# Attention of a hybrid inference step: nine of ten key tiles turned by DMA, the ninth together with the reciprocals

## The reference

```python
C_HEADS = 8; QK_NOPE = 64; QK_ROPE = 32; V_DIM = 64      # 1024 sample keys + 256 cached keys; 128 prompt keys
s  = einsum('bqhd,bkhd->bhqk', q, k) * ATTN_SCALE
pr = softmax(s, axis=-1)
o  = einsum('bhqk,bkhd->bqhd', pr, v)
...
mixed = concatenate([out_a, out_b, o]); x = x + g1 * (mixed @ w_out)
```

## Time and profile before

| | us |
|---|---|
| time, median of 3 runs | 1522.87 (1521.13 to 1523.97) |
| the profiled execution's own time | 1522.13 |
| its span | 1520.2 |
| TensorE busy | 1480.5 |
| VectorE, ScalarE, GpSimd busy | 605.1, 408.0, 280.3 |

### The profile page before, as it was taken

How to read it: one execution, slowest core, us unless ns; L and a number is a source line. 1 busy time by engine, 2 the same in 40 slices (tenths; PEclk the granted TensorE clock), 3 DMA queues, 4 the chain that set the end, 5 groups by cost and what they waited for, 6 DMA issues and landing times.

```text
span 1520.2 us, 25562 instructions
## 1 busy us (share of the span) xinstructions
PE 1480.5 (97%) x10145; PEld 1180.3 (78%) x10145; DVE 605.1 (40%) x1385; ACT 408.0 (27%) x933; POOL 280.3 (18%) x308
## 2 busy tenths in 40 slices
PE   6999999999999999999999999999999999999997
PEld 3654545666666655444899999999999999999996
DVE  2211446676868673136683222222222222222215
ACT  2400102555646452235321111111111111111114
POOL 0005400463747463110000100100000000000000
PEclk9999999999999999999999999999999999999999
DMA  9971001475747593541587999999889989899885
GB/s 364 353 261 50 32 0 41 82 137 104 142 98 144 130 200 73 194 166 70 191 322 271 323 294 312 315 353 300 291 316 296 362 293 300 313 292 357 291 260 223
DMA packets 313917, 338.79 MB, mean 223 GB/s; under 512 B 209091, under 2 KB 210666, under 8 KB 311678
## 3 DMA queue, kind: packets, MB, share of 16 engines
q1 hardware_dynamic: 308814, 319.58, 66.4%
q0 software_dynamic: 4752, 17.30, 4.4%
q10 hardware_dynamic: 288, 1.05, 0.2%
HBM read 266.18 MB, written 21.64 MB: 189 GB/s over the span
## 4 chain that ended last, share of the span: by engine, by line
PE 88%; DVE 5%; DMA 4%; ACT 2%; issue 1%; POOL 0%; SPq 0%; DVEq 0%; ACTq 0%; POOLq 0%
PE ps L1286 32%; PE ps L1315 16%; PE ps L678 8%; PE ps L1016 7%; PE ps L915 6%; PE ps L969 4%; DMA wreg<-wreg 2%; PE ps L703 2%; PE ps L869 2%; PE ps L693 1%; PE ps L894 1%; PE ps L881 1%; DVE stat L1921 1%; PE ps L710 1%; DMA wreg<-x_rows 1%
## 5 line engine op out<-in xcount | busy, mean ns | idle before, releaser
L1286 PE MATMUL ps<-mreg,wreg 128*128 128x144 f32 x4096 | 506.3, 286 | 0.0
L1286 PEld LDWEIGHTS ps<-mreg,wreg 128*128 128x128 f32 x4096 | 503.4, 190 | 0.7 <-ACT hreg L1625 0.4
L1315 PE MATMUL ps<-mreg,wreg 128*128 128x144 f32 x2048 | 256.4, 286 | 2.1 <-DVE mreg L2365 2.1
L1315 PEld LDWEIGHTS ps<-mreg,wreg 128*128 128x128 f32 x2048 | 253.1, 190 | 2.5 <-DVE mreg L2365 2.3
L2365 DVE TENSOR_TENSOR mreg<-ps,mreg 128x144 f32<-128x144 f32 x128 | 39.4, 307 | 357.6 <-PE ps L1286 346.7
L2530 POOL COPY wreg<-hreg 128x1024 uint16<-128x1024 uint16 x128 | 146.2, 1168 | 156.7 <-ACT hreg L1504 156.1
L915 PE MATMUL ps<-wreg 128*128 128x512 f32 (+2 forms) x400 | 159.0, 520 | 3.8 <-ACT hreg L1504 3.7
L1662 ACT ACTIVATE mreg<-ps 128x144 f32<-128x144 f32 x128 | 37.2, 291 | 426.1 <-PE ps L1286 426.1
L1016 PE MATMUL ps<-wreg,mreg 128*128 128x512 f32 x288 | 130.5, 598 | 0.0
L678 PE MATMUL ps<-hreg,wreg 128*128 128x512 f32 (+1 forms) x400 | 128.9, 480 | 0.0
L2577 POOL DMA_INDIRECT x_rows<-hreg,idx_s x15 | 23.9, 1596 | 533.1 <-DVE hreg L2342 521.6
(11 more groups left out here) (310 smaller groups left out, 1217.7 us busy)
## 6 DMA issues: line engine op xcount, KB each, us to landing
wreg<-in_w_e_dram SPq DMA_DIRECT2D x96, 2048.0 KB, 12.4
wreg<-in_w_ada_dram SPq DMA_DIRECT2D x16, 1024.0 KB, 8.3
wreg<-in_w_ada_dram SPq DMA_DIRECT2D x16, 512.0 KB, 10.9
wreg<-in_w_out_dram SPq DMA_DIRECT2D x8, 512.0 KB, 4.2
wreg<-in_x_sample_dram SPq DMA_DIRECT2D x8, 512.0 KB, 4.6
x_rows<-wreg SPq DMA_DIRECT2D x8, 512.0 KB, 3.5
xn_rows<-wreg SPq DMA_DIRECT2D x8, 512.0 KB, 2.6
wreg<-x_rows SPq DMA_DIRECT2D x8, 512.0 KB, 8.5
```

The costliest lines, as they stand in the source:

```text
L1286: mm = pe.matmul(o[:, 0:CAP], w[s][:, k, (f % 4) * P:(f % 4 + 1) * P], xsT[b][:, k, :], start=(k == 0), stop=(k == KD - 1))
L1315: mm = pe.matmul(bank[4 + dm % 2][:, 0:CAP], w2[f // 4][:, f % 4, dm * P:(dm + 1) * P], hidT[:, f, :], start=(f == 0), stop=(f == 7))
```

## The change

- `EXTRA = 1`: of the two key tiles that TensorE turned, tile 8 is now turned by DMA, and TensorE turns tile 9 alone. A third transpose for each query tile (`turn_rest`) carries tile 8 of both heads and, in its last 128 columns (as halves, 256), the spread reciprocals of both. It replaces the product with the identity and its eviction. It has one input buffer (`rest_halves`) and one output buffer (`rest_halves_T`).
- GpSimd splits tile 8 of each head in a third, smaller copy and writes the reciprocals as halves. Before the third copy it waits until the last rest is turned. ScalarE joins the rest (`rest_joined`) behind the exponential of the odd head. `weigh` takes tile 9 first and tile 8 last. `exponential(n)` now waits for the third copy of head `n - 2` too.
- The values of the start of a pass come behind the scores of both first heads, and ScalarE evicts them instead of VectorE.
- Two eighths of `w_out` each are loaded in passes 1 and 2 (behind heads 5 and 9), four in pass 3 (behind heads 2, 5, 8 and 11). The semaphore is shared with the cache's loads.
- The prompt tile's rest (reciprocals only) is issued behind the moves of the next pass's queries.

```diff
-        probT = view(hreg, 2 * KEYS, 4, KEYS)
+        probT = view(hreg, 2 * KEYS, 2, (20 + 1) * P)
-        rec_rows = [view(hreg, 8640 + s * P, P) for s in range(2)]
+        rest_halves = view(hreg, 8640, REST * P).bitcast(U16)
+        rest_halves_T = rt[:, 0, 0:REST * P].bitcast(U16).rearrange("p (c q) -> p c q", q=P)
+        def rest_of(t):
+            return probT[:, t % 2, 16 * P:(16 + REST) * P]
+        def rec_rows(t):
+            return probT[:, t % 2, (15 + REST) * P:(16 + REST) * P]
...
# SyncE
+                if n % 2:
+                    turn_rest(i, n // 2)
+            def turn_rest(i, t):
+                if t:
+                    turn_out(sp, i, t - 1, "rest")
+                sp.wait_ge(halves_split, prob_split(i, 2 * t + 1, 2))
+                sp.dma_start_transpose(out=rest_halves_T, in_=rest_halves).then_inc(rest_turned, 16)
                 for n in range(1, 16):
                     turn_prob(i, n)
+                    if i and n in (5, 9):
+                        w_out_part(2 + 2 * i + n // 9)
                 sp.wait_ge(s_mm, (i + 1) * 18)
                 move_queries(i + 1)
+                turn_rest(i, 8)
...
                 turn_prob(3, n)
-                if n < KD:
-                    sp.dma_start(w_out_sb[:, n, :], w_out[0, n * P:(n + 1) * P, :]).then_inc(w_out_in, 16)
+                if n % 3 == 2 and n < 12:
+                    w_out_part(n // 3)
...
# TensorE
-                for ch in range(3):
-                    score(i, 0, ch)
-                values(i, 0)
-                values(i, 1)
-                for ch in range(3):
-                    score(i, 1, ch)
-                values(i, 2)
+                for n in range(2):
+                    for ch in range(3):
+                        score(i, n, ch)
+                for g in range(3):
+                    values(i, g)
...
-                    for a in range(2 if n < 16 else 1):
-                        kt = 4 * ch + a
+                    for a in range(2 - EXTRA if n < 16 else 1):
+                        kt = 8 + EXTRA + a if n < 16 else 0
-                    for t in range(NT):
-                        if REC_BESIDE[t] == (n, ch):
-                            pe.wait_ge(halves_split, prob_split(i, 2 * t + 1, 2))
-                            mm = pe.matmul(rec_at(t), rec_cols[t % 2], ident, start=True, stop=True)
...
+                        if kt == 8 and EXTRA:
+                            turn_out(pe, i, t, "rest")
...
# ScalarE
-                def rec_evict(t):
-                    turned_by_pe(i, REC_BESIDE[t])
-                    act.activation(rec_rows[t % 2], rec_at(t), ACT.Copy).then_inc(t_out, 1)
+                def rest_joined(t):
+                    act.wait_ge(rest_turned, (i * NT + t + 1) * 16)
+                    act.activation(rest_of(t).bitcast(U16).rearrange("p (c h) -> p h c", h=2),
+                                   rest_halves_T.rearrange("p (h k) q -> p h (k q)", h=2), ACT.Copy).then_inc(t_out, 1)
...
                 exponential(0)
+                values_out(0)
+                values_out(1)
                 exponential(1)
+                values_out(2)
                 for n in range(2, 16, 2):
                     if n >= 4:
                         joined(n - 3, 0)
                     turned(n - 2, 2)
                     if n >= 4:
-                        rec_evict((n - 4) // 2)
                         exponential(n - 1)
+                        rest_joined((n - 4) // 2)
                     exponential(n)
                     turned(n - 1, 2)
                 joined(13, 0)
                 exponential(15)
                 exponential(16)
+                rest_joined(6)
                 turned(14, 2)
-                rec_evict(6)
                 exponential(17)
                 turned(15, 2)
                 joined(15, 0)
+                rest_joined(7)
                 turned(16, 0)
-                rec_evict(7)
                 turned(17, 0)
-                rec_evict(8)
+                rest_joined(8)
...
# GpSimd
+                if i or t:
+                    pool.wait_ge(rest_turned, (i * NT + t) * 16)
+                rest = rest_halves.rearrange("p (h c) -> p h c", h=2)
+                if EXTRA and n < 16:
+                    pool.tensor_copy(rest[:, :, j * EXTRA * P:(j + 1) * EXTRA * P],
+                                     prob[j][:, 8 * P:(8 + EXTRA) * P].bitcast(U16).rearrange("p (k h) -> p h k", h=2))
                 pool.wait_ge(rec_ok, i * 18 + n + 1)
-                pool.tensor_copy(rec_cols[t % 2][:, 64 * j:64 * j + 64],
-                                 a_rec[:, n % 4:n % 4 + 1].to_broadcast([P, 64])).then_inc(halves_split, 1)
+                at = 2 * EXTRA * P + 64 * j
+                pool.tensor_copy(rest[:, :, at:at + 64],
+                                 a_rec[:, n % 4:n % 4 + 1].bitcast(U16).unsqueeze(2).to_broadcast([P, 2, 64])
+                                 ).then_inc(halves_split, 1)
+EXTRA = 1
+REST = 2 * EXTRA + 1
+KEY_ORDER = (9, 0, 1, 2, 3, 4, 5, 6, 7, 8)
```

More of the change, by code:

```diff
@@ L203, in build @@
         prob_halves = [view(wreg, at, 512).bitcast(U16) for at in (6528, 7040, 23232, 23744)]
-        rec_cols = [view(wreg, 24256 + s * P, P) for s in range(2)]
         prob_halves_T = [view(wreg, 16384 + s * 512, 512).bitcast(U16).rearrange("p (c q) -> p c q", q=P) for s in range(4)]
@@ L344, in build @@
         pool_step, diff_ok = sem("pool_step"), sem("diff_ok")
-        cache_in, new_st = sem("cache_in"), sem("new_st")
-        w_out_in = sem("w_out_in")
+        side_in, new_st = sem("side_in"), sem("new_st")
+        CACHE_LOADS = 8
         wq_in, wkv_in, wq_ok = sem("wq_in"), sem("wkv_in"), sem("wq_ok")
@@ L386, in build, with prob_tile @@
         prob_turned = (x_turned, y_turned, sem("odd_turned0"), sem("odd_turned1"))
+        rest_turned = sem("rest_turned")
+        def prob_tile(t, j, kt):
+            if kt < 8:
+                at = 8 * j + kt
+            elif kt < 8 + EXTRA:
+                at = 16 + EXTRA * j + kt - 8
+            else:
+                at = 16 + REST + (2 - EXTRA) * j + kt - 8 - EXTRA
+            return probT[:, t % 2, at * P:(at + 1) * P]
+        def rest_of(t):
+            return probT[:, t % 2, 16 * P:(16 + REST) * P]
+        def rec_rows(t):
+            return probT[:, t % 2, (15 + REST) * P:(16 + REST) * P]
         def prob_split(i, n, h):
@@ L429, in pv_at @@
             return bank[MID_BANK[("weigh", t)]][:, 0:P]
-        def rec_at(t):
-            return bank[MID_BANK[("turn",) + REC_BESIDE[t]]][:, 2 * P:3 * P]
         def turn_out(eng, i, n, ch):
@@ L445, in join_prob @@
             eng.wait_ge(prob_turned[2 * j + part], (i * 8 + t + 1) * 16)
-            return copy(probT[:, 2 * (t % 2) + j, part * 512:(part + 1) * 512].bitcast(U16).rearrange("p (c h) -> p h c", h=2),
+            return copy(probT[:, t % 2, (2 * j + part) * 512:(2 * j + part + 1) * 512].bitcast(U16).rearrange("p (c h) -> p h c", h=2),
                         prob_halves_T[2 * j + part].rearrange("p (h k) q -> p h (k q)", h=2))
@@ L591, in _ @@
                 sp.dma_start(x_again[t], tok_rows(x_sample, x_prompt, t)).then_inc(xa_in[t], 16)
+            turn_rest(3, 8)
             sp.wait_ge(pv_mm, 4 * NT)
@@ L961, in weigh @@
                     turn_out(pe, i, 2 * t + 1, 2 if t < NT - 1 else 0)
-                    for kt in (8, 9, 0, 1, 2, 3, 4, 5, 6, 7) if t < NT - 1 else (10,):
+                    order = KEY_ORDER if t < NT - 1 else (10,)
+                    for kt in order:
                         if kt in (0, 4):
@@ L966, in weigh @@
                             turn_out(pe, i, 2 * t + 1, kt // 4)
+                        if kt == 8 and EXTRA:
+                            turn_out(pe, i, t, "rest")
                         for j in range(2):
-                            src = kt if t < NT - 1 else 0
                             mm = pe.matmul(pv_at(t)[64 * j:64 * j + 64, :], v_sb[:, kt, 64 * j:64 * j + 64],
-                                           probT[:, 2 * (t % 2) + j, src * P:(src + 1) * P],
-                                           start=(kt in (8, 10)), stop=(kt in (7, 10)))
+                                           prob_tile(t, j, kt if t < NT - 1 else 0),
+                                           start=(kt == order[0]), stop=(kt == order[-1]))
                     mm.then_inc(pv_mm, 1)
@@ L1484, in turned @@
                     turned_by_pe(i, (n, ch))
-                    w = 2 * P if n < 16 else P
-                    act.activation(probT[:, 2 * (t % 2) + j, ch * 512:ch * 512 + w], bank[MID_BANK[("turn", n, ch)]][:, 0:w],
+                    w = (2 - EXTRA) * P if n < 16 else P
+                    at = (16 + REST + (2 - EXTRA) * j if n < 16 else 8 * j) * P
+                    act.activation(probT[:, t % 2, at:at + w], bank[MID_BANK[("turn", n, ch)]][:, 0:w],
                                    ACT.Copy).then_inc(t_out, 1)
@@ L1934, in weighed @@
```

(16 more changed lines are left out.)

37 lines of the change are left out of this document (16 added, 21 removed).

## The result

The changed kernel takes 1541.3 us (median; 1533.3 to 1545.2) where the kernel before takes 1523.0 beside it: a ratio of 1.0114, 95% interval 1.0082 to 1.0145. It is slower by about 18 us. The forecast was 1524.0 with a range up to 1531, so it was wrong. The profiled execution is the slowest of the four, 1545.15 us, 23 more than the profiled one of before; so the trace accounts for 23 us, of which the medians show 18.

The account below looks back on a forecast made before the run. It took TensorE as today's bound (7.49 us a tile) and the single rest buffer's loop (7.35) as the new one. Passes +2.2, pass 3 -0.87 and -0.25, loads 0: +1.1 us, 1524.0 against the median; range 1520 to 1527, with rivals 1516 to 1531.

Parts of the forecast that it names:

- The tile: Passes' middle: one query tile takes 7.35 us, against 7.40 now; bounds 7.15 and 7.65.
- The rest's landing: Third transpose of each tile, 768 columns wide: lands in 2.9 us by the slope of wider transposes.
- TensorE's relief: TensorE loses two transposes and one product a tile: 0.43 us, 7.49 to 7.06, no gain by itself in the middle.
- The single buffer: GpSimd's third copy waits until the previous rest is turned; this added loop sets the tile at 7.35 us.
- ScalarE's loop alone: Join to exponential to next join: 7.25 us a tile, 7.15 at best; as a rival 1517.6 us, chance 0.22.
- the price of a load: SP's queue: 0.63 us per output weight load; four moved cost 2.5, pass 3 gains 2.5, 0 in all.
- the rival of the transposes' queue: The transposes' DMA queue becomes the bound, at 7.9 us a tile: 1535.5 us, chance 0.10.
- the pass's end: Last large exponential to next first score: key evictions wait behind two rests, 16.3 us against 15.2, +1.0 to 1.1.
- The third rival: Single rest buffer: 768 columns land like 1024, so the new loop is 7.65 us; 1530.9 us, chance 0.18.
- -0.25 for each of four middles: Five free tiles in each pass, each 0.05 us shorter: -0.25 us a pass.
- the tail: End of pass 3, TensorE-bound: two pairs lose a transpose (0.21) and three products go (0.66), -0.87 us.
- the fourth: Rival: the transposes' queue becomes the bound, 7.9 us a tile, 1535.5 us, chance 0.10.

Follow-up runs that it names:

- keys_before_last_rest: The changed kernel, but ScalarE evicts the next pass's keys before it joins the last rest of a pass: 1530.6 us, ratio 1.0052.
- keys_and_loads_between_passes: The changed kernel with the next keys evicted before the last rest's join and all eight output weight loads issued between the passes: 1520.5 us, ratio 0.9995.

## Why the prediction was wrong

**The tile was right.** Predicted 7.35 with a best case of 7.15, measured 7.15 to 7.5 where nothing else stood in the queue, but for one tile of pass 1 (7.7 to 8.1) that no row explains; the middles of passes 1 and 2 without loads are 44.0 to 44.7, about those of before. The rest's landing, which I named as the first danger, was 2.9 us in the median, the predicted value. Its source line, after:

```profile
DMA to landing us min/median/max: 2.8/2.9/5.0
```

TensorE's relief gave the middles nothing, as worked out from the earlier trace rows. The single buffer, which I took as the new bound, costs 0.4 to 0.8 us a pass. I had 7.15 for ScalarE's loop alone; with two buffers the tile came near it, but the chain of that kernel's pass 2 gives these tiles to TensorE, so that it isn't shown that ScalarE's loop sets them.

**First failed step: "today's 0.63, which a row gives", the price of a load.** The row was misread: of the 5.0 us that I divided by eight, 2.4 were VectorE's preparation of the router weights. The size still lies within what a load costs in the kernel before (0.5 us in passes 1 and 2, 0.3 to 0.75 in pass 3, by whether eight or four stand there). What made the error is the next move: a price read in one kernel was carried into another whose queue the same change had filled. There a load costs 1.8 us in passes 1 and 2, where the upper bound in the text was 1.25, and about 1 in pass 3. Predicted for the four moved loads: 2.5 us longer in passes 1 and 2, 2.5 shorter in pass 3. Measured: +7.2, and +1.3 in pass 3's middle. The rows for it were there: the earlier trace rows gave the DMA share, and the rival of the transposes' queue said "a load or a late issue puts that over 7.35". I gave it 0.10 as a bound on every tile, when it needed to hold only for those with a load.

**Second failed step: the pass's end, "16.3, against 15.2. So +1.0 to 1.1".** The mechanism was right in every link: rest 7, its join, rest 8, its join, then the keys. The size was off: +5.06, +4.21 and +1.68 instead of 1.05 each. The first score came 18.4, 17.6 and 17.0 us after the last large exponential (predicted 16.3). Rest 8 was issued 10.0, 10.6 and 10.4 us after that exponential (predicted 10.0) and landed after 5.0, 3.5 and 3.0 us (predicted 2.9): 1.0 and 2.8 us over three passes. With the predicted 3.2 that makes 7.0 of the 11.0. The landing went in as one number; the words "landings hardly differ among equal transposes (3.0 to 3.2)" pass over the 5.9 at the end of the same row. (The third rival, with its landing of 3.2, also counts +1.3 for an end where the text before it has 1.7 for that landing; this moves its sum by about 1 us and decides nothing.) Almost all of the rest is a link that the prediction left out, the 3.7 us of TensorE's lower clock: I wrote that TensorE "waits there" and charged the wait alone.

The 5.0 us of pass 0 have a row of their own. The DMA queues of the changed kernel, 351 to 358 us:

```profile
DMA  9197949492996925999996999900004989100000
GB/s 342 53 290 158 290 105 343 105 342 53 290 211 132 219 48 92 196 224 177 231 263 138 110 44 48 50 7 9 9 10 83 236 132 217 11 0 0 0 0 0
...
q8 instruction: 1, 0.02, 0.8%
```

Among 40 slices of 0.175 us there are four, from 355.55 us, in which the engines move next to nothing (7 to 10 GB/s), and about 1 us ahead of them one fetch of instructions starts. The transpose on its way lands late. In the five of the seven kernels with the wide rest and one buffer in which such a fetch starts 2.2 to 2.6 us behind the issue of this rest, it lands after 4.9 to 5.0 us; in the two in which the fetch starts ahead of the issue (keys_before_last_rest and keys_and_loads_between_passes) after 2.9 and 3.0. No run moves the fetch alone, so this is a match in time and not a cause shown. The same is seen in pass 0's middle, where two to four tiles of over 8 us stand in nearly every profile, of before too (8.13 and 8.32 there). That pass's middle took 45.9 to 48.7 in three profiles of kernels without the change and 46.9 to 50.3 in those with it; what part of the +3.64 the change has stays open. The profile that I read happened to show the shortest of them.

**What the sum missed.** Predicted +1.1; measured +18.3 of the medians. The 23 of the two profiles are the ends' 11.0, the 8.5 of the three middles with loads, and the 3.6 of pass 0's middle. Undoing the key order and the loads' places takes it back to the kernel before (a ratio of 0.9995, 0.9985 to 1.0004). The other terms of the sum, -0.25 for each of four middles and -0.87 for the tail, make -1.9 us. Against the kernel before with its loads moved likewise (1520.2) the 1520.5 shows no such gain, but the two intervals are too wide to rule it out. The chances put 0.28 on slower; the mechanism of the third rival (the rest's landing) didn't happen, that of the fourth did, in part of the tiles.

## What to carry to other kernels

A price read from a row holds for the slack that the row's kernel had: where a change adds transfers to a queue, first work out how much idle time the queue has left in one turn of the loop, then put every other transfer into it, and move those that don't fit to where the queue is idle. Before an excess of one stage over another is divided among its obvious causes, look down every engine's timeline for work that only that stage has. And a wait of the engine that sets the pace is charged with what it does to that engine's clock too; in this kernel two short unused products put into the wait kept the clock up there and cost nothing that showed.

## What the hardware showed that was not expected

- TensorE's granted clock fell to the lower level (1.2 GHz, from 2.4) behind waits of 2.20 and 3.15 us between passes and stayed there for some 3.5 us. Behind waits of 1.76 and 1.18 us there it did not fall. Elsewhere it fell behind two waits of 1.02 and 0.74 us close together, and stayed up behind one of 2.32, so the length of a single wait doesn't decide.
- Around the fetch of one 16 KB block of instructions the DMA engines that carry the transposes moved next to nothing for about 0.7 us, and the transpose on its way landed after 5.0 us instead of 2.9; the same late landing goes with such a fetch in four other kernels here.
- A load of 512 KB among transposes occupied the 16 DMA engines for about 2 us in the changed kernel (two loads: 41.8 against 37.5 us) and in the one before (35.8 against 32.0), whether or not it delayed anything.
